# Two latent tails cut 1 + 3 blocks instead of 2 + 2, with PEER's row gathers in a new order

## The chip, the cores and the metric

One NeuronCore of one Trainium2 chip runs the whole program. The metric is the device time of that core in microseconds (us), as the median of several executions. The profile is one further execution, recorded instruction by instruction.

## What is computed

Two layers of a backbone run over 512 latent tokens and 256 context tokens, 1024 channels, all in fp32. Cut to what matters here:

```
for l in range(2):
    o_lat, o_ctx = token_mixer(modulate(x), modulate(ctx), ...)   # conv, retention, mLSTM, windowed attention
        # merge: acc = sum_i sigmoid(gate_i) * (ys[i] @ w_branch[i]);  out = acc @ w_out
    x = x + ga1 * o_lat
    x = x + ga2 * peer_ffn(modulate(x, norm2_g[l], sh2, sc2), ...)
    if l == 0: ctx = the same for ctx
return rmsnorm(x, final_g)

def peer_ffn(h, wq, keys, u, v):           # blocks of 128 tokens
    q = h @ wq                             # 8 heads x 2 halves x 128
    s = q . keys                           # 128 keys for each half
    top 16 per half -> 256 candidates -> top 16 experts per head (of 16384)
    act  = gelu(h . u[expert])             # 128 rows of u for each token
    out += (gate * act) @ v[expert]        # 128 rows of v for each token
```

## The kernel before

A block is 128 tokens: the context has two, the latents four. The program is four passes through the mixer, one after the other: `C0` (layer 0, context), `L0` (layer 0, latents), `C1` (layer 1, context, states only) and `L1` (layer 1, latents). `C0`, `L0` and `L1` end in PEER calls `PC0` (2 blocks, numbered 0 and 1), `PL0` (4 blocks, 2 to 5) and `PL1` (4 blocks, 6 to 9).

**The tail.** Behind the mixer's branches stands a tail of three stages, `merge`, `out` and `query`, done for one half of the blocks at a time: `halves_of(p)` (L73) gives `(0, 1), (2, 3)` for latents, and `pass_stages` makes stages `merge0, out0, query0, merge1, out1, query1`. `merge_part` (TensorE L1174) goes over 16 pairs (j, branch). Each pair has a gate weight (1 MB) and a branch weight (512 KB), and for both of its column halves m eight gate matmuls (L1182) and four branch matmuls (L1188) with the half's tokens as the moving operand, W = 256 columns. `outp` (L1196) multiplies each block with four 1 MB weights (L1216), adds the residual, makes the second RMSNorm (VectorE and ScalarE), stores the normalised rows `h2`, and transposes them. `query` (L1227) makes 16 chunks of the query (L1236, eight matmuls of 256 columns, 1 MB of weight for two chunks) and the scores (L1249). An fp32 matmul leaves two records in the trace. Weights come in through one queue (SyncE, L3039) into a ring of 4 slots; a slot is loaded again when TensorE has used it. All weights of the tail are read once for each half, 16 x 1.5 + 4 + 8 = 36 MB.

In `l0` twelve of the sixteen pairs of `merge0` are woven with the late convolution (`late_units`), in `l1` twelve with the attention (`attn_mix`); the last four are the stage itself.

**Routing.** The scores of a half's first block in `query0` are searched at once by VectorE (`top_keys`, `candidates`, two heads behind each group of four chunks). The scores of the other blocks go to memory, and VectorE searches them a head at a time between the dot products of the PEER block before (`route_part`, L2142). `centre`, `pick_keys` and `experts` then make the indices.

**PEER.** A block has 128 slots (`SLOTS`). For each slot GpSimd issues a gather of 128 rows of `u` and one of 128 rows of `v` (L3009), 4 KB a row, 512 KB in all. VectorE makes one dot product for each `u` gather (L2197). TensorE sums each `v` gather into PSUM with four narrow matmuls (`v_sum`, L1266 to L1275, eight records). `gather_tables` (L112) gives each gather one of 8 row buffers, and of 14 from the second block of a latent call on (6 of them lie in the mixer's memory), and says which reader must be done before. The order is, for `it` from the first block to one behind the last: slot by slot, `u` of block `it` and `v` of block `it - 1`. So the first 128 steps gather `u` alone, the last 128 `v` alone.

**What runs beside what.** Each engine's program is one fixed list. `side_by_side` (L725) puts steps of the PEER call between the pieces of another generator, in proportion to the cost that this yields (TensorE's estimates):

```
side_by_side("l0", mixer(L0), side, ROUTE + 3 * SLOTS, 0.9, costs)   # side = peer(PC0)
side_by_side("t0", tail(L0, 1), side, ROUTE + SLOTS, 1.0, costs)     # side = peer(PL0)
side_by_side("c1", mixer(C1), side, 3 * SLOTS, 1.0, costs)
side_by_side("t1", tail(L1, 1), side, ROUTE + SLOTS, 1.0, costs)     # side = peer(PL1)
```

`ROUTE` = 4 steps stand for the last part of routing. `mixer(L0)` and `mixer(L1)` end with their tail of half 0. GpSimd isn't part of these lists: it goes through the gathers in their order and waits for buffers, for the indices of a block (`idxu`, `idxt`), and once for the end of `query1` before `u` of a call's second block. `L1`'s mixer starts when `PL0` has ended.

Of the kernel before, what the change touches and what calls it, by code (L numbers as in the profile page):

```python
# [72 lines left out]
def halves_of(p):  # L73

    return [(x, x + 1) for x in range(0, p.n // P, 2)]
# [35 lines left out]

def gather_tables():  # L112

    buffer, before = {}, {}
    for call in (PC0, PL0, PL1):
        last, reader = call.first + len(call.blocks) - 1, {}
        for it in range(call.first, last + 2):
            if it == call.first:
                u_ring, v_ring = range(8), ()
            elif it == last + 1:  # L120
                u_ring, v_ring = (), range(8 if call is PC0 else 14)
            elif call is PC0:
                u_ring, v_ring = (0, 1, 2, 3), (4, 5, 6, 7)
            else:
                u_ring, v_ring = (0, 1, 2, 3, 8, 9, 10, 11), (4, 5, 6, 7, 12, 13)
            for n in range(SLOTS):
                for kind, ring, i, step in (("u", u_ring, it, "dot"), ("v", v_ring, it - 1, "v_summed")):
                    if call.first <= i <= last:
                        x = ring[n % len(ring)] if len(ring) in (4, 8, 14) else ring[((it - call.first) * SLOTS + n) % 6]
                        buffer[kind, i, n], before[kind, i, n] = x, reader.get(x)  # L130
                        reader[x] = (step, i, n)
    return buffer, before
# [3 lines left out]
ROUTE = 4  # L136
# [159 lines left out]
def query_units(p, f):  # L296

    order = []
    for c in range(2 * HEADS):
        order.append(("chunk", c))  # L300
        if f == 0 and c % 4 == 1 and c > 4:
            order.append(("score", 0, c // 4 - 1))
    if f == 0:
        order.append(("score", 0, 3))
    return order + [("score", x, g) for x in halves_of(p)[f][1 if f == 0 else 0:] for g in range(4)]
# [44 lines left out]
def build(nc, ins, out, known):  # L350
    ctx = ExitStack()
    with ctx:
# [189 lines left out]
        ACC, H2, XO = lay(4 * BB * LAT, KD * W, 2 * D, 2 * D)  # L542
        ACC, H2, XO = rows4(ACC, KD), rows4(H2, 2), rows4(XO, 2)
        GS, PRD = H2[:, 0, 0:3 * W].rearrange("p (b t) -> p b t", b=3), H2[:, 0, 3 * W:4 * W]
        ODD = MA[:, 0:4 * BB * LAT].rearrange("p (c f t) -> p c f t", c=16, f=2)

        def out_work():

            ga, sc2, sh2, g2 = (ODD[:, 4 * x:4 * x + 4, 0, :] for x in range(4))
            return ga, sc2, sh2, g2, g2[:, 0:2, :]  # L550

        H2T = HT.rearrange("p (k f t) -> p k f t", k=KD, f=2)[:, :, 0, :]

        def query_rows(c):
            return ACC[:, c, :] if c < KD else H2[:, (c - KD) // 4, (c - KD) % 4 * W:(c - KD) % 4 * W + W]

        def score_work(x):

            if x == 0:
                return SCO.rearrange("p (g c t) -> p g c t", g=4, c=2)  # L560
            if x == 2:
                return ODD[:, 0:8, 1, :].rearrange("p (g c) t -> p g c t", g=4)
            return MA[:, 10 * D + 2 * D:10 * D + 4 * D].rearrange("p (g c t) -> p g c t", g=4, c=2)
# [184 lines left out]
        def _(eng):  # L748
# [425 lines left out]
            def merge_part(p, f, part):  # L1174
                pn, half = p.name, slice(f * W, (f + 1) * W)
                for j, i_ in part:
                    wg = weight(("gate", pn, f, j, i_))
                    wb = weight(("branch", pn, f, j, i_), BB)
                    for m in range(2):
                        b = bank(("gate", pn, f, j, i_, m))  # L1180
                        for k in range(KD):
                            i = mm(b[:, 0:W], wg[:, k, m * P:(m + 1) * P], HTk(p)[:, k, half], start=(k == 0),  # L1182
                                   stop=(k == KD - 1))
                        i.then_inc(*mn.step("full", ("gate", pn, f, j, i_, m)))
                        yield 3.4
                        b = bank(("branch", pn, f, j, i_, m))
                        for k in range(BB):
                            i = mm(b[:, 0:W], wb[:, k, m * P:(m + 1) * P], YS(p, i_)[:, k, half], start=(k == 0),  # L1188
                                   stop=(k == BB - 1))
# [4 lines left out]
                        yield 1.8  # L1194

            def outp(p, f):  # L1196
                mn.stage((f"out{f}", p.name))
                pn = p.name

                def transposed(x, t):  # L1200

                    for half in range(2):
                        b = bank(("hT", pn, t, half))
                        eng.wait_ge(*at("h2", pn, t))
                        for k in range(4):
                            kk = half * 4 + k
                            i = turn(b[:, k * P:(k + 1) * P], H2[:, x % 2, kk * P:(kk + 1) * P], ident)
                        i.then_inc(*mn.step("full", ("hT", pn, t, half)))

                for x in halves_of(p)[f]:  # L1210
                    t = blocks_of(p)[x]
                    for j in range(D // W):
                        w = weight(("out", pn, f, j))
                        b = bank(("out", pn, j, t))
                        for k in range(KD):
                            i = mm(b[:, 0:W], ACC[:, k, x % 2 * P:(x % 2 + 1) * P], w[:, k, :], start=(k == 0), stop=(k == KD - 1))  # L1216
                        i.then_inc(*mn.step("full", ("out", pn, j, t)))
                        if x % 2:
                            used(("out", pn, f, j))
                        yield 3.5  # L1220
                    if x % 2:
                        transposed(x - 1, t - 1)
                        yield 2.2
                transposed(x, t)
                yield 2.2

            def query(p, f):  # L1227
                mn.stage((f"query{f}", p.name))
                pn = p.name
                for what, *n in query_units(p, f):  # L1230
                    if what == "chunk":
# [3 lines left out]
                        for k in range(KD):  # L1235
                            i = mm(b[:, 0:W], w[:, k, m * P:(m + 1) * P], H2T[:, k, :], start=(k == 0), stop=(k == KD - 1))  # L1236
# [3 lines left out]
                        yield 3.5  # L1240
                        continue
                    x, g = n
                    t = blocks_of(p)[x]
                    b = bank(("score", pn, t, g))
                    for y in range(4):
                        hc = 4 * g + y
                        if x % 2 == 0:
                            eng.wait_ge(*at("read", ("wq", pn, f, hc)))
                        i = mm(b[:, y * KEYS:(y + 1) * KEYS], query_rows(hc)[:, x % 2 * P:(x % 2 + 1) * P],  # L1249
# [1938 lines left out]
```

## Time and profile before

| | |
|---|---|
| median of 3 runs | 6093.1 us (6083.96 to 6100.71) |
| time of the profiled execution | 6088.19 us |
| its span, first to last instruction | 6086.3 us |
| busy: TensorE / VectorE / GpSimd / ScalarE | 4101.5 / 3226.0 / 2754.4 / 702.4 us |
| mean granted TensorE clock | 0.763 |
| gathers | 2560, 1384.49 MB, 60.1% of the 16 DMA engines' span |
| `merge0` of `l0`; of `l1` (with attention) | 1583 to 1848; 4103 to 4373 |
| window `t0`; the rest of `PL0` beside `C1` and alone | 1974 to 2320; 2320 to 3592 |
| window `t1`; the rest of `PL1` alone | 4494 to 4844; 4844 to 6066 |

Busy time is the sum over an engine's instructions without overlaps. The DMA share is the mean busy share of the core's 16 DMA engines and can come out slightly over 1. A granted clock of 1.00 is 2.4 GHz, 0.50 is 1.2 GHz. In a timeline row, the number in brackets is the engine's idle time before the group and what ended it.

### The profile page before, as it was taken

The numbers are of one execution on the slowest core, as the hardware profiler recorded it, in microseconds if no ns is written. First come the engines' busy times: TensorE is split into PE (matmuls) and PEld (weight loads), VectorE is DVE, ScalarE is ACT, GpSimd is POOL, SyncE is SP. The second block draws the span as 40 slices with busy tenths as digits, with TensorE's granted clock in tenths as the row PEclk, the third lists the DMA queues.
The fourth block names the chain that finished last, engine by engine and source line by source line (L and its number), as shares of the span: only waits on it lengthen the run. The fifth ranks groups of instructions, "written<-read, shape, count | busy, mean of one in ns | idle before, by whom it ended". The sixth has DMA issues, their size and how long they took to land. (4 is left out here: it accounts for less than half of the span.)

```text
span 6086.3 us, 64932 instructions
## 1 busy us (share of the span) xinstructions
PE 4101.5 (67%) x23632; PEld 2449.2 (40%) x23632; DVE 3226.0 (53%) x7722; ACT 702.4 (12%) x1562; POOL 2754.4 (45%) x2606
## 2 busy tenths in 40 slices
PE   5889676668998885554454569898878633334447
PEld 4767544335566663221021125457767500000001
DVE  3522698657434875756544217443268665664430
ACT  1221112123111001000000011233100100000000
POOL 0000144566330445777777730000014477777775
PEclk9999787779999987665555679999989855555555
DMA  6655466899885899999999961112559899999999
GB/s 224 207 164 179 156 234 227 303 322 335 275 293 188 311 331 332 386 363 402 384 400 409 404 269 51 52 46 73 161 190 333 322 379 364 395 378 397 409 402 380
DMA packets 721230, 1739.23 MB, mean 286 GB/s; under 512 B 88912, under 2 KB 371408, under 8 KB 719248
## 3 DMA queue, kind: packets, MB, share of 16 engines
q0 software_dynamic: 380032, 1384.49, 60.1%
q1 hardware_dynamic: 314896, 304.03, 16.0%
q10 hardware_dynamic: 25984, 46.56, 2.2%
q8 instruction: 188, 3.08, 0.2%
q14 instruction: 130, 1.06, 0.1%
HBM read 1706.98 MB, written 27.89 MB: 285 GB/s over the span
## 5 line engine op out<-in xcount | busy, mean ns | idle before, releaser
L3009 POOL DMA_INDIRECT arena<-in_peer_u,arena x1280 | 1408.2, 1100 | 2259.4 <-DVE arena L2107 1093.7
L1275 PE MATMUL bank<-arena 128*32 128x256 f32 x10240 | 1199.9, 563 | 1348.5 <-DMA arena<-in_peer_v,arena 1339.7
L2197 DVE CUSTOM_DVE_ANT_0 arena<-arena 128x1024 f32<-128x1024 f32 x1280 | 1540.6, 1222 | 908.6 <-DMA arena<-in_peer_u,arena 885.6
L3009 POOL DMA_INDIRECT arena<-in_peer_v,arena x1280 | 1319.4, 1031 | 627.7 <-issue 310.9
L1275 PEld LDWEIGHTS bank<-arena 128*32 128x32 f32 x10240 | 252.0, 131 | 2250.6 <-DMA arena<-in_peer_v,arena 2135.9
L784 PE MATMUL bank<-arena 128*128 128x512 f32 (+1 forms) x1856 | 731.6, 550 | 27.9 <-issue 13.1
L1182 PE MATMUL bank<-arena 128*128 128x256 f32 x2560 | 620.3, 398 | 89.0 <-issue 56.2
L1182 PEld LDWEIGHTS bank<-arena 128*128 128x128 f32 x2560 | 506.8, 200 | 184.7 <-issue 99.6
L784 PEld LDWEIGHTS bank<-arena 128*128 128x128 f32 x1856 | 372.8, 206 | 338.2 <-issue 315.0
L1188 PE MATMUL bank<-arena 128*128 128x256 f32 x1280 | 306.6, 382 | 2.3 <-ACT arena L2736 2.3
L1236 PE MATMUL bank<-arena 128*128 128x256 f32 x1280 | 290.1, 390 | 17.8 <-issue 17.8
L1236 PEld LDWEIGHTS bank<-arena 128*128 128x128 f32 x1280 | 249.7, 196 | 55.1 <-issue 19.7
L1188 PEld LDWEIGHTS bank<-arena 128*128 128x128 f32 x1280 | 239.1, 190 | 47.8 <-ACT arena L2736 12.7
L754 PE MATMUL bank<-arena 128*128 128x128 f32 x408 | 94.3, 359 | 219.7 <-DVE arena L1434 123.9
L1965 DVE SCALAR_TENSOR_TENSOR arena<-arena,bank 128x256 f32<-128x256 f32 x120 | 50.3, 419 | 328.2 <-PE bank L1188 293.0
L1507 DVE SCALAR_TENSOR_TENSOR arena<-arena 128x512 f32<-128x512 f32 (+1 forms) x360 | 213.8, 658 | 5.8 <-DVE arena L1507 0.4
L795 PE MATMUL bank<-arena 128*128 128x256 f32 (+1 forms) x960 | 214.9, 384 | 1.4 <-ACT arena L2522 1.4
L2819 ACT ACTIVATE arena<-arena 128x16 f32<-128x16 f32 x80 | 17.2, 216 | 1628.8 <-DVE arena L2197 1571.5
L795 PEld LDWEIGHTS bank<-arena 128*128 128x128 f32 x960 | 180.5, 207 | 38.6 <-issue 16.0
L2167 DVE TENSOR_TENSOR arena<-bank,arena 128x512 f32<-128x512 f32 x20 | 12.9, 685 | 338.3 <-PE bank L1275 338.3
L754 PEld LDWEIGHTS bank<-arena 128*128 128x128 f32 x408 | 64.7, 185 | 259.5 <-issue 169.3
L2971 POOL DMA_DIRECT2D arena<-in_mod_w x20 | 15.0, 755 | 323.1 <-PE bank L822 323.1
(269 smaller groups left out, 3844.5 us busy)
## 6 DMA issues: line engine op xcount, KB each, us to landing
arena<-in_w_in SPq DMA_DIRECT2D x152, 1024.0 KB, 6.9
arena<-in_mod_w POOLq DMA_DIRECT2D x20, 2048.0 KB, 11.5
arena<-in_peer_wq SPq DMA_DIRECT2D x40, 1024.0 KB, 5.5
arena<-in_w_branch SPq DMA_DIRECT2D x60, 512.0 KB
arena<-in_w_out SPq DMA_DIRECT2D x20, 1024.0 KB, 6.8
arena<-in_peer_u,arena POOLq DMA_INDIRECT x1280
arena<-in_peer_v,arena POOLq DMA_INDIRECT x1280
arena<-in_w_branch SPq DMA_DIRECT2D x40, 256.0 KB
```

Of the source, the lines that this page charges most:

```text
L754: return nc.tensor.transpose(dst, src, eye)
L784: i = mm(b[:, 0:p.n], w[:, k, m * P:(m + 1) * P], HTk(p)[:, k, :], start=(k == 0), stop=(k == KD - 1))
L795: i = mm(b[:, 0:n], HTk(p)[:, k, t * P:(t + 1) * P], w[:, k, c0:c0 + n], start=(k == 0), stop=(k == KD - 1))
L1182: i = mm(b[:, 0:W], wg[:, k, m * P:(m + 1) * P], HTk(p)[:, k, half], start=(k == 0), stop=(k == KD - 1))
L1188: i = mm(b[:, 0:W], wb[:, k, m * P:(m + 1) * P], YS(p, i_)[:, k, half], start=(k == 0), stop=(k == BB - 1))
L1236: i = mm(b[:, 0:W], w[:, k, m * P:(m + 1) * P], H2T[:, k, :], start=(k == 0), stop=(k == KD - 1))
L1275: i = mm(banks[6 + g // 2][32 * j:32 * j + 32, (g % 2) * W:(g % 2 + 1) * W], G["ws"][:, g, 32 * m:32 * m + 32], G["row"][ROW_BUFFER["v", i ...
L1507: v.scalar_tensor_tensor(y[:, m, :], cp[:, m, j:j + p.n], tap, y[:, m, :], ALU.mult, ALU.add)\
L1965: v.scalar_tensor_tensor(PRD, g, 1.0, b[:, 0:W], ALU.add, ALU.mult).then_inc(*mn.step("read", ("branch", pn, f, j, i_, m)))
L2197: v.tensor_tensor_reduce(u, u, G["h2"][it % 2], 1.0, 0.0, ALU.mult, ALU.add, G["dots"][:, n:n + 1]).then_inc(*pr.step("dot", it, n))
L2819: act(G["act"][:, hs], G["dots"][:, hs], ACT.Gelu).then_inc(*pr.step("gelu", it, h))
L3009: fl.done(eng.indirect_dma_start(G["row"][x], None, table, bass.IndirectOffsetOnAxis(ids[:, n:n + 1], 0)), f"row_landed{x}", (kind + "_lan ...
```

## The change

1. `halves_of` gives `(0,)` and `(1, 2, 3)` for the latent passes. The moving operand of merge and query is 128 columns wide in half 0 and 384 in half 1; the context pass keeps its one half of 256. `query_units` now puts the scores of each half's first block between the chunks, so VectorE searches two blocks (0 and 1) in the query stages, and `route_part` only blocks 2 and 3.
2. `peer_steps` writes PEER's order out as a list. For a latent call: 4 routing steps; 128 `u` of the first block; its first 64 `v` alone; 32 more `v`, every eighth with a routing step of the second block; 128 `u` of the second block with a `v` of the first at every fourth; then `u` of a block and `v` of the one before, as until now. In `t0` and `t1` 4 + 128 + 64 steps stand beside the tail instead of 4 + 128, in `c1` 32 + 384 instead of 384. `PC0` keeps its order.
3. The row buffers follow: 8 for `u` and `v` alike until the 96th `v`, then 8 and 6.
4. The memory of the tail is laid out anew (`tail_rows`), and the modulation rows and the first residual block are loaded ahead of the end of the merge (`out_rows_early`), the rest behind it (`out_rows_late`).

```diff
 def halves_of(p):
-    return [(x, x + 1) for x in range(0, p.n // P, 2)]
+    return [(0,), tuple(range(1, p.n // P))] if p.t0 else [tuple(range(p.n // P))]
...
+V_EARLY, V_LEAD = SLOTS // 2, SLOTS // 4
+def led(call):
+    return (call.first,) if call is PC0 else (call.first, call.first + 1)
+def peer_steps(call):
+    first, last, steps = call.first, call.first + len(call.blocks) - 1, []
+    for s in range(ROUTE):
+        steps.append(((first, s), None, None))
+    for n in range(SLOTS):
+        steps.append((None, (first, n), None))
+    if call is not PC0:
+        for n in range(V_EARLY):
+            steps.append((None, None, (first, n)))
+        for n in range(V_LEAD):
+            s, now = divmod(n, V_LEAD // ROUTE)
+            steps.append((None if now else (first + 1, s), None, (first, V_EARLY + n)))
+        for n in range(SLOTS):
+            v, now = divmod(n, 4)
+            steps.append((None, (first + 1, n), (first, V_EARLY + V_LEAD + v) if now == 3 else None))
+    for it in range(led(call)[-1] + 1, last + 2):
+        for n in range(SLOTS):
+            steps.append((None, (it, n) if it <= last else None, (it - 1, n)))
+    return steps
...
-                            i = mm(b[:, 0:W], wg[:, k, m * P:(m + 1) * P], HTk(p)[:, k, half], start=(k == 0),
+                            i = mm(b[:, 0:n], wg[:, k, m * P:(m + 1) * P], HTk(p)[:, k, half], start=(k == 0),
...
-                        yield 3.4
+                        yield n / W * 3.4
...
-            side_by_side("t0", tail(L0, 1), side, ROUTE + SLOTS, 1.0, costs)
+            side_by_side("t0", tail(L0, 1), side, ROUTE + SLOTS + V_EARLY, 1.0, costs)
-            side_by_side("c1", mixer(C1), side, 3 * SLOTS, 1.0, costs)
+            side_by_side("c1", mixer(C1), side, V_LEAD + 3 * SLOTS, 1.0, costs)
-            side_by_side("t1", tail(L1, 1), side, ROUTE + SLOTS, 1.0, costs)
+            side_by_side("t1", tail(L1, 1), side, ROUTE + SLOTS + V_EARLY, 1.0, costs)
...
+            def out_rows_early(p, f):
+                T, first_it = tail_rows(p, f), CALLS[p.name].first
+                ended = STAGES[STAGES.index((f"merge{f}", p.name)) - 1]
+                for e in ENG:
+                    eng.wait_ge(*at("end", e, ended))
+                eng.wait_ge(*at("mod_stored", p.l, 1))
+                eng.wait_ge(*at("experts", first_it if f else first_it - 1))
+                dma(T["ga"], mod_piece(p, 2), "out_gate", ("out_gate", p.name, f))
+                residual_in(p, f, halves_of(p)[f][0])
+                dma(T["g2"], norm_row(p), "out_rows")
+                if f == 0:
+                    dma(T["sc2"], mod_piece(p, 4), "out_rows")
+                    dma(T["sh2"], mod_piece(p, 3), "out_rows", ("out_rows", p.name, f))
```

## Rows read from the trace of the kernel before

**Rows 1.** The page's part 5: line, engine, operation | busy us, mean ns of one.

```profile
L2197 DVE CUSTOM_DVE_ANT_0 arena<-arena 128x1024 f32<-128x1024 f32 x1280 | 1540.6, 1222 | 908.6 <-DMA arena<-in_peer_u,arena 885.6
```

**Rows 2.** Busy time by stretch (us): each engine (instructions), granted clock, DMA share, GB/s.

```profile
730.00:1080.00 350.00, 250.22 (x806) 152.62 (x804) 296.51 (x764) 63.71 (x124) 150.07 (x125) 0.82 0.68 233
1080.00:1505.00 425.00, 311.76 (x2131) 177.89 (x2133) 263.83 (x610) 100.57 (x224) 268.56 (x253) 0.83 0.93 329
...
1583.00:1848.00 265.00, 264.49 (x1606) 172.31 (x1607) 116.42 (x189) 21.71 (x45) 95.58 (x95) 1.00 0.87 289
...
1974.00:2320.00 346.00, 281.96 (x1235) 241.97 (x1235) 266.45 (x621) 33.92 (x73) 150.10 (x128) 0.90 0.93 326
...
4103.00:4315.00 212.00, 188.40 (x1290) 161.59 (x1289) 65.83 (x169) 64.43 (x171) 0.00 (x0) 0.98 0.24 75
...
4373.00:4414.00 41.00, 30.89 (x145) 26.77 (x145) 15.24 (x28) 5.07 (x9) 0.00 (x0) 0.92 0.84 282
4414.00:4494.00 80.00, 67.05 (x320) 59.58 (x320) 45.02 (x208) 7.84 (x16) 0.00 (x0) 0.91 0.33 106
4494.00:4716.00 222.00, 186.67 (x769) 157.98 (x769) 181.75 (x464) 15.66 (x39) 97.84 (x84) 0.90 0.92 318
...
4844.00:5190.00 346.00, 130.24 (x965) 24.47 (x969) 206.39 (x482) 4.38 (x10) 271.50 (x245) 0.50 0.99 374
5190.00:5893.00 703.00, 285.14 (x2107) 53.44 (x2107) 385.70 (x779) 7.13 (x21) 540.00 (x527) 0.50 1.02 397
```

**Rows 3.** Timeline of GpSimd's gathers where `t0` and `t1` end and at each call's end.

```profile
2325.84 0.94 POOL L3009 DMA_INDIRECT arena<-in_peer_v,arena  x1 [0.30 <-issue]
...
3576.21 0.93 POOL L3009 DMA_INDIRECT arena<-in_peer_v,arena  x1 [0.30 <-issue]
...
4842.86 0.94 POOL L3009 DMA_INDIRECT arena<-in_peer_u,arena  x1 [10.70 <-ACTq L2803]
4844.10 0.94 POOL L3009 DMA_INDIRECT arena<-in_peer_v,arena  x1 [0.30 <-issue]
...
6050.48 0.93 POOL L3009 DMA_INDIRECT arena<-in_peer_v,arena  x1 [0.30 <-issue]
```

**Rows 4.** Timeline of TensorE, matmuls of 256 and of 128 columns in layer 1's tails.

```profile
4140.03 2.05 PE L1137 MATMUL bank<-arena 128*128 128x128 f32 x16 [1.29 <-ACT arena L2698]
...
4436.42 1.05 PE L1249 MATMUL bank<-arena 128*128 128x128 f32 x8
4437.31 7.94 PE L1236 MATMUL bank<-arena 128*128 128x256 f32 x36
...
4580.63 3.62 PE L1182 MATMUL bank<-arena 128*128 128x256 f32 x16
4584.08 1.89 PE L1188 MATMUL bank<-arena 128*128 128x256 f32 x8
```

**Rows 5.** TensorE's groups in 1583 to 1848, and its waits in 1080 to 1505.

```profile
L1275 PE MATMUL bank<-arena 128*32 128x256 f32 x760 | 55.7, 388 | 0.0
...
PE bank L1275 <- DMA arena<-in_peer_v,arena: 84.4, 46, 5.2
```

**Rows 6.** Weight loads: issues in 4110 to 4375 (with queue) and 4494 to 4713, us to landing.

```profile
q1 hardware_dynamic: 24468, 24.50, 30.8%
...
arena<-in_w_in SPq DMA_DIRECT2D x14, 1024.0 KB, 5.4
...
arena<-in_w_in SPq DMA_DIRECT2D x14, 1024.0 KB, 10.0
```

**Rows 7.** Timeline of VectorE: one routing group in `query0`, then the indices behind it.

```profile
4438.20 0.49 DVE L2020 MAX8 arena<-arena 128x8 f32<-128x128 f32 x2 [1.16 <-ACT arena L2793]
...
4450.43 0.42 DVE L2118 COPY arena<-bank 128x256 f32<-128x256 f32 x1
...
4498.64 0.23 DVE L2062 TENSOR_TENSOR arena<-arena 128x128 f32<-128x128 f32 x1
...
4515.97 0.23 DVE L2092 CAST arena<-arena 128x128 uint32<-128x128 f32 x1
```

More of the change, by code:

```diff
@@ L115, in gather_tables @@
     for call in (PC0, PL0, PL1):
[L116 to L123, printed above, removed]
-            else:
[L125 to L131, printed above, removed]
+        last, reader, given = call.first + len(call.blocks) - 1, {}, {"u": 0, "v": 0}
+        for _, u, v in peer_steps(call):
+            if call is PC0:
+                u_ring = range(8) if u and u[0] == call.first else (0, 1, 2, 3)
+                v_ring = (4, 5, 6, 7) if u else range(8)
+            elif u and u[0] == call.first or v and v[0] == call.first and v[1] < V_EARLY + V_LEAD:
+                u_ring, v_ring = range(8), range(8)
+            else:
+                u_ring = (0, 1, 2, 3, 8, 9, 10, 11)
+                v_ring = range(14) if v and v[0] == last else (4, 5, 6, 7, 12, 13)
+            for kind, row, ring, step in (("u", u, u_ring, "dot"), ("v", v, v_ring, "v_summed")):
+                if row:
+                    x = ring[given[kind] % len(ring)]
+                    given[kind] += 1
+                    buffer[(kind,) + row], before[(kind,) + row] = x, reader.get(x)
+                    reader[x] = (step,) + row
     return buffer, before
 ROW_BUFFER, READ_BEFORE = gather_tables()
-ROUTE = 4
 CONST = {}
@@ L1174, in merge_part @@
             def merge_part(p, f, part):
-                pn, half = p.name, slice(f * W, (f + 1) * W)
+                pn, half, n = p.name, span(p, f), width(p, f)
                 for j, i_ in part:
@@ new lines, in peer @@
+                for lead, u, v in peer_steps(call):
+                    if lead:
+                        it, s = lead
+                        if s == 0 and it > call.first:
+                            rows_in(it)
+                        if s == 2:
+                            gate_exp(pr, G, it)
+                    if u:
+                        it, n = u
+                        h, k = divmod(n, TOPK)
+                        if k == TOPK - 1:
+                            gelu(it, h)
+                        if it + 1 <= last and it + 1 not in led(call):
+                            if n == (HEADS - 2) * TOPK:
+                                gate_exp(pr, G, it + 1)
+                            if n == 0:
+                                scores_in(it + 1)
+                            if n == 4:
+                                rows_in(it + 1)
+                        if n == SLOTS - 1:
+                            spread(it)
+                    if v:
+                        it, n = v
+                        if n == 2 and it > call.first:
+                            x_out(it - 1)
+                        if n == 24:
+                            x_in(it)
+                    yield 0
@@ L2998, in gathers @@
                 G = peer_work(call)
-                last = call.first + len(call.blocks) - 1
                 def gather(kind, it, n):
```

409 lines of the change are left out of this document (211 added, 198 removed).

## The prediction

> **What bounds the kernel now.** I cut the span into stages with the table of busy time by stretch, read what bounds each, then went to the timelines of TensorE, GpSimd and VectorE for prices. Three regimes appear [rows 2]. In PEER alone (4844 to 5893) the DMA share is 0.99 to 1.02 while TensorE is busy for 38 to 41% at half clock: the gathers' bytes set the pace. From the first `v` gather behind `t1` to the last 895 intervals lie in 6050.48 - 4844.10 = 1206.4 us, 1.348 us each; in layer 0 it is 1250.4 us, 1.397 each, beside `C1`'s weights [rows 3]. In `merge0` of layer 0 TensorE is busy for 264.5 of 265 us. In `t0` and `t1` both are nearly full: DMA 0.92 to 0.93, TensorE 81 to 84% [rows 2]. In layer 1's `merge0` no gather runs, DMA share 0.24. So a gather row taken out of the stretches behind the tails is worth 1.348 us, provided that the tails don't grow by as much. Both layers are symmetrical here: `L1` starts when `PL0` has ended, and the program ends with `PL1`.
>
> **Part 1, matmul widths.** TensorE's pitch at full clock: 16 records of 256 columns take 4584.08 - 4580.63 = 3.45 us, 0.216 each; 8 records of 128 columns take 0.89 us, 0.111 each [rows 4]. So time goes with columns; 384 I take as 0.322 (256 plus half of it). A half has 16 x 2 x 12 x 2 = 768 merge records, 16 x 8 x 2 = 256 query records, 64 `out` records for each block. Half 0 loses 768 x 0.105 + 256 x 0.105 + 64 x 0.216 = 81 + 27 + 14 = 122 us of TensorE; half 1 gains the same. Widths alone are neutral.
>
> The Trainium skill (TensorE: Matmul & The Clock Gate, Back-to-back issue gap) says otherwise for narrow matmuls: with a weight load for each, 128 columns sustain about 81 ns instead of an isolated 56. By that ratio the 1024 narrow records would cost 1024 x 0.111 x 0.45 = 51 us a layer. The trace's 0.111 already has a weight load for each record, so I go by the trace; that rule's outcome is rival 3.
>
> **Part 2, half 0 gets shorter.** How much of the 122 us arrives?
> - Layer 1, twelve pairs woven with attention: 12 x 48 x 0.105 = 60 us less TensorE work over 16 units. But TensorE already waits 1.29 us for ScalarE's exponential in a unit [rows 4], and that chain doesn't shrink. A unit is about 13 us now (212 / 16, rows 2); the scores are issued one unit ahead of the transposes that wait, so the chain from scores to probabilities is about as long as a unit, 13 us. With only 4 us of merge and 3.3 of attention of TensorE's own in a unit, two units can't be shorter than 13 + 3.3 + 4, one not than about 10. I take 40 us, bounds 20 and 60.
> - The last four pairs: 20 us less; but a pair of 1.5 MB must land in the 5.3 us of the pair before, and 1 MB alone takes 5.4 us [rows 6]. 18 us.
> - `out`: 14 us less; four weights are needed in 14 us, behind 2.5 MB of early rows. I take 8, bounds 0 and 14.
> - `query`: 27 us less for TensorE, but VectorE's search of two heads is 4450.43 - 4438.20 = 12.2 us [rows 7] and four chunks are now only 7.1 us. The stage becomes six chunks, then 4 x 12.2 us and some copies: about 63 us of 80 [rows 2]. 17 us.
> Sum for layer 1: 83 us earlier. In layer 0 the woven pairs are TensorE-bound, so all 81 us come; its window "l0" also gets 17% denser in PEER steps (388 steps over about 700 units of yielded cost instead of 820, counted in the code), so some 49 `v` sums at 55.7 / 95 = 0.59 us [rows 5] leave `merge0`. With what DMA (0.87 there) takes back I count 93, with `out` 10 and `query` 17: 120. Against it stands the place that the steps move to: 1080 to 1505, DMA 0.93, would shrink to 363 us and can't get under 0.93 x 425 / 0.98 = 403; with VectorE at 85% ahead of it [rows 2] I charge 33 us, bounds 0 and 60. Layer 0: 87 us earlier.
>
> **Part 3, `t0` and `t1` get longer.** TensorE's pure work now: 768 + 256 + 128 records at 0.216 and some 100 narrow ones = 260 of 350 us; 90 us are overhead. After: 768 x 0.322 + 192 x 0.216 + 256 x 0.322 + 144 x 0.111 = 247 + 41 + 82 + 16 = 386, and 64 `v` sums x 0.59 = 38: 424. Of the overhead these stay: the start behind the routing (12), the last block's norm (17), half-clock stretches (8; 0.90 over 222 us now, rows 2), a new wait of 7 where the first `v_sum` stands in TensorE's list until the last dots are weighed, turned and spread; and late weights. Those shrink: a weight lands in 10.0 us here instead of 5.4 [rows 6], a pair of TensorE work was 10.4 us and becomes 15.5. I take 12. Sum 56, the window 480 us, +130. DMA has for it 200 gathers x 1.348 = 270 and 36 MB at 24.5 MB in 0.308 x 265 us [rows 6] = 120 and some rows: 400 of 480, no denser than now. Bounds 445 and 520. VectorE loses the routing of the second block there (about 50 us, see below) and gets it back in `query1`, 12.2 us for each 20.6 us of chunks: hidden. The residual and modulation loads behind `merge1` are hidden by the first block's 14 us of `out`.
>
> **Part 4, what is left behind the tails.** GpSimd doesn't stop at the end of `t1` any more (10.70 us idle now, rows 3): 64 `v` are summed, 8 more in buffers, so 824 of 1024 gathers remain instead of 896: 72 x 1.348 = 97 us less in each call. The 24 `v` left before `u` of the second block cover 32 us; `centre` to `experts` needs 4516.2 - 4498.6 = 17.6 us [rows 7]. Hidden, if the search of its last heads ends with `query1`. Without that cover the 10.7 us gap returns.
> The second block's `u` now go with only a quarter of `v`: 160 gathers, 216 us. VectorE has in it all that it has in 4844 to 5190 now, 206 us [rows 2]: 128 dots at 1.23 [rows 1] and about 50 us of routing in lumps of up to 8 us. At 0.96 of the pace, with 8 buffers of `u`, I charge 20 us; in layer 0, where `C1` adds some 0.1 us a step, 22. Bounds 0 and 50.
>
> **The sum.** Layer 1: -83 + 130 - 97 + 20 = -30. Layer 0: -87 + 130 - 97 + 22 = -32. Together -62 on 6088.2, the profiled execution; that stands 5 us under the median of 6093.1. Forecast **6031 us**, own range 5995 to 6070.
>
> **Rivals.**
> 1. *Only bytes count.* The windows grow to 455 only (wide matmuls hide every weight, `v` sums fill waits), and VectorE's lumps vanish in the buffers. -25 x 2 - 42: **5939 us**. For it: of VectorE's 908.6 us idle ahead of dots 885.6 are put down to gathers not landed [rows 1], so it has mostly been ahead of them. Against: it has been so at 60% of the pace, not at 96%.
> 2. *VectorE and the pace of steps take it back* (the change does nothing). In the second block's `u` part the dots fall behind their buffers by 50 instead of 21 us in each call: +58, **6089 us**. For it: no such dense part exists today. Against: the 885.6 us of rows 1.
> 3. *Narrow matmuls cost what the page has.* 51 us a layer in half 0, none given back in half 1: **6133 us**. For it only that rule; against it 0.111 against 0.216 [rows 4].
> 4. *`v` sums stop the mixer.* In `t0` and `t1` each `v_sum` stands in TensorE's list ahead of the tail's matmuls. If the gathers, held back by the weights, are always the later ones, each costs a full 1.348 instead of 0.59: +49 in each window, **6129 us**. From 31 us a window (0.48 us a sum) it eats the gain. For it: 84.4 us of such waits in 1080 to 1505 [rows 5], 155 sums, 0.54 each. Against: there two gathers fall on a step, here one, on a step of over 2 us.
>
> **Chances.** Forecast 0.46, rival 1 0.31, rival 2 0.12, rival 3 0.02, rival 4 0.09. A measurement of this kernel tells 0.3% (18 us) from no change. Faster by more: the forecast and rival 1 nearly whole, 0.77; within 0.3%: rival 2 and the forecast's edge, 0.12; slower: rivals 3 and 4, 0.11. The range for 8 in 10 leaves out rivals 3 and 4, the far end of 1 and a sliver of 2: 5940 to 6095.
>
> **What would show it.** The first `u` gather of `PL1` near 4400 (the indices come at 4516.2 now [rows 7], less 83 and 32); with less, part 2 is wrong. `t1` of about 480 us with a DMA share of 0.8 to 0.9 and hardly a wait for weights in `merge1`; waits of the `v` matmuls on DMA there mean rival 4. A continuous row of gathers across the end of `query1`. Some 236 us instead of 216 for the second block's `u`, with VectorE full. Then the old pace of 1.35 us a gather. The prediction is wrong above all if half 0's 120 us don't arrive, or if the window grows by 160 rather than 130.

## The result, and the profile after

The changed kernel took 6158.24 us (median of 4, 6152.26 to 6170.6), the kernel before beside it 6090.83 (4 runs): ratio 1.0112, 95% interval 1.009 to 1.0134. It is 67 us slower where 62 us faster was forecast. The profiled execution has a span of 6150.5 us against 6086.3, 64.2 more.

Busy time by stretch of the changed kernel; columns as in [rows 2]:

```profile
1046.00:1473.00 427.00, 294.00 (x1669) 153.92 (x1670) 231.84 (x529) 70.12 (x140) 268.65 (x254) 0.75 0.92 328
1473.00:1666.00 193.00, 167.42 (x1566) 102.60 (x1564) 71.19 (x163) 64.09 (x161) 81.84 (x85) 1.00 0.75 258
1666.00:1849.00 183.00, 163.25 (x1253) 116.63 (x1246) 111.60 (x193) 17.86 (x44) 51.16 (x45) 0.96 0.84 283
1947.00:2442.00 495.00, 442.13 (x1850) 264.16 (x1850) 268.31 (x602) 40.90 (x79) 221.62 (x199) 0.95 0.87 305
2442.00:3670.00 1228.00, 586.19 (x4034) 199.15 (x4034) 642.13 (x1411) 51.57 (x106) 888.39 (x825) 0.57 0.97 371
2512.00:2787.00 275.00, 100.71 (x498) 60.35 (x490) 222.84 (x546) 20.15 (x38) 197.73 (x160) 0.63 0.89 328
4183.00:4383.00 200.00, 166.73 (x1559) 155.51 (x1557) 67.64 (x191) 66.67 (x185) 0.00 (x0) 0.97 0.43 135
...
4407.00:4477.00 70.00, 39.11 (x288) 38.27 (x288) 43.71 (x208) 4.62 (x12) 0.00 (x0) 0.77 0.33 106
4477.00:4771.00 294.00, 259.92 (x762) 150.46 (x763) 184.98 (x326) 19.20 (x41) 150.49 (x122) 0.93 0.87 304
...
4851.00:4977.00 126.00, 125.34 (x753) 70.32 (x754) 45.85 (x208) 10.52 (x19) 46.20 (x50) 0.98 0.76 250
...
5017.00:5262.00 245.00, 39.11 (x302) 7.64 (x298) 205.99 (x490) 4.40 (x10) 192.36 (x161) 0.51 0.94 345
```

The stage borders in both traces give this account, in us, with the terms of the prediction beside it:

| | before | after | moved | forecast |
|---|---|---|---|---|
| start of `t0` (first gate matmul of half 1) | 1974 | 1947 | -27 | -87 |
| window `t0` | 346 | 495 | +149 | +130 |
| rest of `PL0`, beside `C1` and alone | 1272 | 1228 | -44 | -75 |
| `L1`'s mixer to its first gate matmul | 511 | 513 | +2 | 0 |
| layer 1, `merge0` to `query0` | 391 | 294 | -97 | -83 |
| window `t1` | 350 | 500 | +150 | +130 |
| rest of `PL1` to its last sum | 1222 | 1153 | -69 | -77 |
| **sum** | | | **+64** | **-62** |

So layer 1 gained 14 us, and layer 0 lost 78. Of the 126 us between forecast and measurement 60 are in the first row, 39 in the two windows and 31 behind `t0`; layer 1's other rows are 6 us better than forecast, and `L1`'s mixer took 2 more. In the first row the miss begins here: the first gate matmul of layer 0 comes at 1666.2 instead of 1582.9, 83 us later, though nothing in that part of the mixer was changed.

### The profile page after: what moved, and what is told of

Read it like the earlier page. It is cut to its first block and busy times, and to the rows that moved or that the text cites. A ratio compares the mean times of both kernels' runs of the same rounds, so it can differ in the third digit from the quotient of the medians.

```text
span 6150.5 us, 64955 instructions
## 1 busy us (share of the span) xinstructions
PE 4066.5 (66%) x23632; PEld 2300.8 (37%) x23632; DVE 3230.0 (53%) x7724; ACT 713.8 (12%) x1569; POOL 2797.5 (45%) x2606
## 5 line engine op out<-in xcount | busy, mean ns | idle before, releaser
L3065 POOL DMA_INDIRECT arena<-in_peer_u,arena x1280 | 1440.0, 1125 | 2104.2 <-DVE arena L2156 1014.6
L1325 PE MATMUL bank<-arena 128*32 128x256 f32 x10240 | 1153.7, 548 | 1388.1 <-DMA arena<-in_peer_v,arena 1381.9
L1231 PE MATMUL bank<-arena 128*128 128x384 f32 (+2 forms) x2560 | 618.2, 397 | 115.4 <-issue 72.8
L1231 PEld LDWEIGHTS bank<-arena 128*128 128x128 f32 x2560 | 430.4, 200 | 289.2 <-issue 139.0
L833 PEld LDWEIGHTS bank<-arena 128*128 128x128 f32 x1856 | 366.7, 203 | 345.3 <-issue 324.2
L1286 PE MATMUL bank<-arena 128*128 128x128 f32 (+2 forms) x1280 | 306.1, 401 | 19.0 <-issue 16.9
L1237 PE MATMUL bank<-arena 128*128 128x128 f32 (+2 forms) x1280 | 307.8, 384 | 1.8 <-ACT arena L2785 1.8
L1286 PEld LDWEIGHTS bank<-arena 128*128 128x128 f32 x1280 | 216.4, 206 | 100.8 <-issue 35.8
L1237 PEld LDWEIGHTS bank<-arena 128*128 128x128 f32 x1280 | 209.2, 192 | 86.2 <-ACT arena L2785 9.3
L2014 DVE SCALAR_TENSOR_TENSOR arena<-arena,bank 128x128 f32<-128x128 f32 (+2 forms) x120 | 50.5, 421 | 347.0 <-PE bank L1237 201.8
L844 PEld LDWEIGHTS bank<-arena 128*128 128x128 f32 x960 | 179.8, 206 | 38.3 <-issue 15.9
L2218 DVE TENSOR_TENSOR arena<-bank,arena 128x512 f32<-128x512 f32 x20 | 12.9, 686 | 342.0 <-PE bank L1325 342.0
L1266 PE MATMUL bank<-arena 128*128 128x256 f32 x640 | 147.8, 390 | 19.6 <-DMA arena<-in_w_out 17.2
```

Source lines behind the costliest of these rows:

```text
L833: i = mm(b[:, 0:p.n], w[:, k, m * P:(m + 1) * P], HTk(p)[:, k, :], start=(k == 0), stop=(k == KD - 1))
L844: i = mm(b[:, 0:n], HTk(p)[:, k, t * P:(t + 1) * P], w[:, k, c0:c0 + n], start=(k == 0), stop=(k == KD - 1))
L1231: i = mm(b[:, 0:n], wg[:, k, m * P:(m + 1) * P], HTk(p)[:, k, half], start=(k == 0), stop=(k == KD - 1))
L1237: i = mm(b[:, 0:n], wb[:, k, m * P:(m + 1) * P], YS(p, i_)[:, k, half], start=(k == 0), stop=(k == BB - 1))
L1266: i = mm(b[:, 0:W], T["acc"][:, k, y * P:(y + 1) * P], w[:, k, :], start=(k == 0), stop=(k == KD - 1))
L1286: i = mm(b[:, 0:N], w[:, k, m * P:(m + 1) * P], T["h2t"][:, k, :], start=(k == 0), stop=(k == KD - 1))
```

## The experiments

Runs 1 to 4 were on a chip where the kernel before took 6087 us; the other eight where it took 6305 to 6307 us and a gather behind the tails about 1.47 us instead of 1.35. Ratios are always to the kernel before on the same chip, and whole times are compared on one chip alone. The lengths of the windows `t0` and `t1` are compared across chips below: run 9, on the slower one, has 494 and 500 us from the first gate matmul to the last score, the same as the changed kernel on the faster. Where no ratio is given there is one time.

**1. The old density of the context call in the changed kernel.** The number behind the steps is the share of the window over which they are spread: a smaller one sets them denser.

```diff
-            side_by_side("l0", mixer(L0), side, ROUTE + 3 * SLOTS, 0.9, costs)
+            side_by_side("l0", mixer(L0), side, ROUTE + 3 * SLOTS, 1.0, costs)
```

> The changed kernel, but PEER's steps of the context call are spread over the whole of the window l0 (share 1.0) instead of 0.9 of it. The yielded cost of that window is 778.4 units (912.2 before the change), so 388 steps over 778 units are nearly as thin as the old 388 over 821. My theory (the shorter tail squeezed the context call's gathers into a stretch that DMA already filled, which cost some 50 of the 60 us by which t0 starts later than forecast): t0's first merge matmul moves from 1947 to 1895-1925 and the whole gets 25 to 50 us faster than the changed kernel, ratio to the kernel before 1.003 to 1.008. Rival (the narrow tail itself is what arrives late, because of weights or of attention-like chains): t0 starts at 1940-1965, no gain or a loss, as v sums now fall into the tail. Second rival: v sums in tail 0 eat it, also no gain.

6136.89 us, ratio 1.008 (1.0056 to 1.0105). The first gate matmul came at 1623 instead of 1666, but `t0` started at 1936, 11 us ahead of the changed kernel and not 22 to 52: `merge0` took 198 instead of 183 us and `out0` and `query0` 114 instead of 98, since the `v` sums had moved there. The direction is that of the theory, the size at `t0` is under its range; the ratio is at the upper end of its range, and its interval overlaps that of the changed kernel. Of the 43 us gained ahead of the gates 32 were lost again in the tail, as the second rival had it.

**2. The new density in the kernel before, and nothing else.**

```diff
-            side_by_side("l0", mixer(L0), side, ROUTE + 3 * SLOTS, 0.9, costs)
+            side_by_side("l0", mixer(L0), side, ROUTE + 3 * SLOTS, 0.768, costs)
```

> The kernel before, with the share of window l0 lowered from 0.9 to 0.768, so that the context call's steps stand as densely as in the changed kernel (388 steps over 700 units of cost), nothing else. If the density costs 50 to 80 us ahead of the merge, merge0 of layer 0 starts at 1630-1665 instead of 1583, and part of that comes back in a merge with fewer v sums: t0 starts 15 to 50 us later than 1974 and the ratio is 1.003 to 1.008. If the density is harmless (rival): merge0 starts at 1583-1600 plus the v sums moved (25 us), t0 at 1965-1980 and the ratio is 0.998 to 1.001.

6153.9 us, ratio 1.0115 (1.0086 to 1.0143): as slow as the whole change, with old halves and old order, and beyond the 1.003 to 1.008 that I expected. Busy time by stretch of this kernel, columns as above:

```profile
1052.00:1479.00 427.00, 289.41 (x1669) 150.18 (x1670) 231.88 (x531) 70.03 (x140) 272.32 (x254) 0.75 0.91 328
1479.00:1675.00 196.00, 171.86 (x1566) 105.30 (x1564) 71.02 (x163) 64.10 (x161) 80.81 (x85) 0.97 0.75 254
1675.00:1908.00 233.00, 231.92 (x1256) 166.72 (x1249) 118.85 (x193) 21.24 (x44) 46.65 (x45) 1.00 0.68 219
```

The reader is to set its first row against the changed kernel's first (the same 427 us and 1669 records) and against 1080 to 1505 in [rows 2]: 425 us as well, the same 253 gathers, but 2131 TensorE records. The stretch in which the context call gathers `u` and `v` together took its 426 us here whether 2131 or 1669 records of TensorE stood in it. What the mixer doesn't get done there is done behind it: 196 us to the first gate matmul (at 1675) instead of 78. The first 128 `u` gathers end 27 us sooner (319 us from 733 instead of 346), so the gates come 92 us late and not 118. `merge0` gives 30 us of that back (233 instead of 262 to 265), as it has fewer sums. `t0` starts at 2033, 59 us late. TensorE's waits for `v` rows in the stretch from 1052 to 1479, to be set against [rows 5]:

```profile
PE bank L1275 <- DMA arena<-in_peer_v,arena: 125.3, 61, 7.1
```

**3. The second block's lead steps ahead of `C1`'s mixer.** GpSimd's timeline of the changed kernel behind `t0`, and VectorE's at the same place:

```profile
2442.12 0.94 POOL L3065 DMA_INDIRECT arena<-in_peer_v,arena  x1 [0.71 <-issue]
2470.49 0.94 POOL L3065 DMA_INDIRECT arena<-in_peer_v,arena  x1 [27.44 <-PE bank L1325]
```

```profile
2457.49 0.24 DVE L1464 SCALAR_TENSOR_TENSOR arena<-arena 128x8 f32<-128x8 f32 x2 [16.46 <-DMA arena<-mod_rows]
```

The gathers stop for 27 us: the next `v` sum is listed behind `C1`'s first norm, and that waits for the layer's vectors. I took this wait for a new one. It isn't: the kernel before stops at the same place.

```profile
2361.78 1.44 POOL L3009 DMA_INDIRECT arena<-in_peer_v,arena  x1 [20.70 <-PE bank L1275]
```

```diff
+            for _ in range(V_LEAD):
+                next(side)
-            side_by_side("c1", mixer(C1), side, V_LEAD + 3 * SLOTS, 1.0, costs)
+            side_by_side("c1", mixer(C1), side, 3 * SLOTS, 1.0, costs)
```

> The changed kernel, but the 32 v-only steps with the second block's routing stand ahead of C1's mixer instead of between its pieces (c1 then takes 3*SLOTS steps). Theory: in the changed kernel GpSimd stands still for 27 us behind t0, because its next v sum is listed behind C1's first norm, which waits for the layer's vectors (16.5 us of VectorE waiting on mod_rows); with the steps ahead of it the gathers go on, u of the second block starts at about 2490 instead of 2512 and the whole gets 10 to 28 us faster than the changed kernel, ratio 1.0065 to 1.0095. Rival: the vectors' loads come late anyhow and C1's norm then blocks the dense u part instead: the gap is only moved, ratio 1.010 to 1.012.

6152.86 us, ratio 1.0099 (1.0069 to 1.013), which doesn't tell it from the changed kernel. In the traces `u` of the second block starts at 2481 instead of 2512, but from the end of `t0` to the last `v` gather it is 1205 us instead of 1215. Of 31 us at the gap 10 arrive at the end: most of it was only moved, as the rival said. In its trace the `u` gathers now stop behind VectorE's dots, which the norm holds back:

```profile
2511.99 1.14 POOL L3071 DMA_INDIRECT arena<-in_peer_u,arena  x1 [18.55 <-DVE arena L2248]
```

**4. The new order with the old halves.** `peer_steps` without the early search: 64 `v` behind the first 128 `u`, then a `v` at every second `u` of the second block.

```diff
+        for n in range(V_EARLY):
+            steps.append((None, None, (first, n)))
+        for n in range(SLOTS):
+            v, now = divmod(n, 2)
+            steps.append((None, (first + 1, n), (first, V_EARLY + v) if now else None))
...
-            side_by_side("t1", tail(L1, 1), side, ROUTE + SLOTS, 1.0, costs)
+            side_by_side("t1", tail(L1, 1), side, ROUTE + SLOTS + V_EARLY, 1.0, costs)
```

> The kernel before with its two halves of two blocks each, and of the change only the new order: 64 v of the first block stand in t0 and t1 behind its u, and the other 64 go with u of the second block, one at every second slot. No early search of the second block. Sum from the rows: windows t0 and t1 get 64 v sums (0.5 to 0.6 us each, 32 to 38 us) and the wait of 7 us at the first of them, 40 to 50 us longer each; behind them 72 gathers fewer, 97 us less each. If the loss of the change lies in the 1+3 cut (my theory), this one is faster than the kernel before: 0.983 to 0.993. If v sums and gathers in the tails are what costs (rival), the windows grow by 80 or more and the ratio is 0.997 to 1.005.

6119.83 us, ratio 1.0069 (1.0042 to 1.0095). I had expected 0.983 to 0.993. My theory of the 1 + 3 cut as the only culprit fell. Both windows, from the first gate matmul to the last score, grew from 339 and 342 to 433, by 91 to 94 us for 64 sums, or 1.4 to 1.5 us each, and behind them 69 and 91 us were saved.

**5. The same with light weights.** Is it the weights' DMA? Of the gate, `out` and query weights of half 1 only an eighth is loaded; the kernel computes with stale values in their place.

```diff
+        for n, (name, parts) in enumerate(PLAN):
+            if name[1] in ("l0", "l1") and name[0] in ("gate", "out", "wq") and name[2] == 1:
+                (dst, src), = parts
+                PLAN[n] = (name, [((lambda w, dst=dst: dst(w)[:, 0:1, :]), src[:, 0:1, :])])
```

> order_alone (2 + 2 blocks, 64 early v), but in half 1 of both latent tails the gate, out and wq weights are loaded to one eighth only, so that part of the computation uses stale weights: the weights' DMA in t0 and t1 falls from 36 MB to about 11.5 MB. If DMA sets the 433 us of these windows (200 gathers x 1.348 = 270 and 120 us of weights, DMA nearly full), they fall to 340-370 us. If TensorE's own work and its waits for v sums set them (298 us of pure work), they stay above 400.

6295.23 us against 6306.9. The windows were still 420 and 422 us instead of 433. So the loading of the weights is worth 11 to 13 of the 91 to 94 us. TensorE's waits in `merge1` of layer 1, first with full, then with light weights (us in total, times, longest):

```profile
PE bank L1209 <- DMA arena<-in_w_branch: 29.2, 5, 9.1
PE bank L1209 <- DVE arena L1991: 18.5, 6, 5.6
```

```profile
PE bank L1213 <- DVE arena L1995: 40.2, 16, 5.7
```

The waits for weights go, and those for VectorE, which has to free the banks, take their place. It is busy there for 232.5 of 261 us with full and 222.4 of 249 with light weights, because 196 instead of 132 steps over the same tail bring the 128 dots, with the second block's search between them, into less of it.

**6. The early `v` behind the windows, in the changed kernel.**

```diff
-            side_by_side("t0", tail(L0, 1), side, ROUTE + SLOTS + V_EARLY, 1.0, costs)
+            side_by_side("t0", tail(L0, 1), side, ROUTE + SLOTS, 1.0, costs)
-            side_by_side("c1", mixer(C1), side, V_LEAD + 3 * SLOTS, 1.0, costs)
+            side_by_side("c1", mixer(C1), side, V_EARLY + V_LEAD + 3 * SLOTS, 1.0, costs)
```

> The changed kernel with the same list of PEER steps, but only 4 + 128 of them stand in t0 and t1; the 64 early v follow behind (in c1's window for layer 0, alone for layer 1). Theory A (a v in the tail costs PE and DMA time of the tail nearly as much as it saves behind): windows 45 to 75 us shorter than 495 and 500, the rest 86 us longer, in all 0 to 30 us slower than the changed kernel for both layers: ratio 1.010 to 1.017. Theory B (TensorE's fixed order makes each early v cost more than its 1.348 us, as order_alone's 91 us for 64 hint): windows over 86 us shorter, the whole 0 to 30 us faster than the changed kernel, ratio 1.005 to 1.011.

Ratio 1.01 (1.0083 to 1.0117), no different from the changed kernel. The windows are 423 and 425 us (first gate matmul to last score) instead of 494 and 500: 71 and 75 us for 64 `v`, 1.1 to 1.2 us each, which is theory A. `merge1` of layer 1 with the early `v` behind, to be set against 4477 to 4771 in the windows of the changed kernel above:

```profile
4573.00:4830.00 257.00, 249.13 (x762) 146.15 (x763) 140.16 (x247) 18.82 (x38) 90.48 (x84) 0.98 0.82 270
```

No `v` sum stands in either. The changed kernel's 37 us more go with 122 instead of 84 `u` gathers in the merge: TensorE's waits put down to issue, which is where late weights show (run 8), are 33.8 us there and 7.7 here, and the granted clock is 0.93 there and 0.98 here. The other half of the price lies in `out1` and `query1`.

**7. The cut alone.** PEER in its old order, the second block searched in `query1`, its last routing in four steps without gathers.

```diff
+    if call is not PC0:
+        for s in range(ROUTE):
+            steps.append(((first + 1, s), None, None))
+    for it in range(first + 1, last + 2):
```

> The 1 + 3 cut alone: PEER in its old order (128 u, then u and v slot by slot), but the second block is searched in query1, and its last routing (4 steps, 18 us) stands between the first 128 u and the rest with no gathers beside it. t0 and t1 carry 4 + 128 steps. Windows 430 to 455 us (386 of TensorE's pure work and 45 to 70 of pauses) instead of 346 and 350; tail 0 of layer 1 95 us shorter as in the changed kernel, of layer 0 only 27 because of the dense l0 window; behind the windows the old 1272 and 1222 plus 10 to 20 us for the routing gap. Sum: layer 0 +70 to +90, layer 1 +0 to +25: ratio 1.011 to 1.019. If it is no slower than the changed kernel (1.0112), the early v brought nothing.

Ratio 1.0099 (1.0082 to 1.0116); windows 422 us both, shorter than my 430 to 455. `t0` starts at 1959 for 1958 in run 6. The cut without any early `v` is as slow as the whole change: the early `v` brought nothing on balance. But it has a loss of its own: without `v` gathers to cover the second block's last routing, GpSimd stands still for 50.1 us in layer 0 and 38.7 in layer 1 (15.0 and 10.7 in the kernel before), where I had charged 10 to 20 us more.

**8. Light weights in the changed kernel.** The edit is that of run 5, put at the same place:

```diff
+            if name[1] in ("l0", "l1") and name[0] in ("gate", "out", "wq") and name[2] == 1:
+                PLAN[n] = (name, [((lambda w, dst=dst: dst(w)[:, 0:1, :]), src[:, 0:1, :])])
```

> The changed kernel, with gate, out and wq weights of half 1 of both latent tails loaded to one eighth only (that part then computes with stale weights). The changed kernel's windows were 495 and 500 us, in t1 TensorE idle 57 us of it, 46 put down to weights and to issue. If late weights are what lengthens them over my 480, they fall to 445 to 465. If not (order_light had stayed at 420 of 433), they stay above 485.

6233.07 us against 6304.59. The windows (to the last score) fell to 449 and 448 from 494 and 500. TensorE's first stretch of `t1` then is 247 us busy of 247, at full clock: the 768 x 0.322 us of the prediction. With full weights it is 294 us, 260 of them busy: the 47 us between are 34 of waiting and 13 of matmuls at a lower clock (granted 0.93 instead of 1.00). Behind the longest of these waits, 8.62 us, the next 16 records took 7.34 us instead of 5.16.

```profile
4520.00:4767.00 247.00, 247.00 (x764) 145.30 (x764) 185.09 (x325) 19.38 (x42) 145.42 (x122) 1.00 0.87 303
```

**9. Early sums with one narrow matmul of four.**

```diff
-                    for j in range(COLS):
+                    for j in range(1 if it in (PL0.first, PL1.first) and n < V_EARLY and 0 < m < 31 else COLS):
```

> The changed kernel, but of the first 64 v gathers of the latent calls 60 are summed with one of the four narrow matmuls (three quarters of their sum are left out); gathers and waits stay. v_late showed that each early v lengthens the window by 1.16 us. If TensorE's own time for the sums is it (0.5 to 0.6 us, of which three quarters go), the windows fall by 20 to 27 us to 468-480. If it is the wait for the rows or the paced order, they fall by less than 10.

6329.33 us against 6304.59. The windows stayed at 494 and 500 us. But it says nothing against TensorE's time, as the groups of `query1` show, changed kernel first:

```profile
L1325 PE MATMUL bank<-arena 128*32 128x256 f32 x401 | 27.0, 385 | 0.0
```

```profile
L1325 PE MATMUL bank<-arena 128*32 128x256 f32 x112 | 26.1, 385 | 0.0
```

112 records instead of 401 take nearly the same time: the four matmuls of a sum run beside each other, so leaving three out frees nothing. In the timelines the matmul behind a single sum starts 0.57 us after it with all four (4964.50 to 4965.07) and 0.55 with one (5059.94 to 5060.49). This test could not tell the two theories apart.

**10. and 11. The kernel before with a thinner context call.** If density costs, less of it should pay.

```diff
-            side_by_side("l0", mixer(L0), side, ROUTE + 3 * SLOTS, 0.9, costs)
+            side_by_side("l0", mixer(L0), side, ROUTE + 3 * SLOTS, 1.0, costs)
```

> The kernel before with the share of window l0 raised from 0.9 to 1.0: 912 / 388 = 2.35 units of mixer cost to a PEER step instead of 2.12. Runs so far fit a simple rule: the context call's first 260 steps (to its last u) take 770 us whatever stands between them (last u at 1473 to 1505 in five kernels), so what the mixer hasn't done by then comes behind, at about 1 us a unit. By that rule 260 x 0.24 = 61 units more are done by then: merge0 starts at 1525-1550 instead of 1583, v sums fall into out0 and query0 and cost 15 to 30 us there, and t0 starts 15 to 45 us ahead of 1974: ratio 0.993 to 0.998. Rival (the old share is at the bend, further thinning stretches the gathers themselves): u ends after 1530, t0 at 1965-1985, ratio 0.999 to 1.002.

> before_l0_thin once more, beside the kernel above and on another chip, since its first chip was 3.5% slower in all kernels: 0.992 to 0.997 if the gain isn't bound to that chip; 0.998 to 1.001 if the slower gathers there made it.

Ratios 0.9943 (0.9923 to 0.9963) and 0.9979 (0.9967 to 0.9991): faster both times, by 0.2 to 0.6%. The second ratio is above my 0.992 to 0.997, and both came at the slower pace of the gathers, so that neither says whether the gain is bound to it; only run 1, in the changed kernel, points the same way on the faster chip. The last `u` gather moved to 1557 and 1559 and the stretch to 452 us, so it isn't as rigid as my rule had it (1473 to 1519 in all the others but run 12's, and 442 us for the stretch in run 1), but the first gate matmul comes at 1562 to 1563 instead of 1610 (run 5, the same window `l0`, at the same pace).

**12. Layer 1 of the changed kernel, layer 0 of the kernel before with the thin call.** The core of the edit, against the changed kernel:

```diff
-    return [(0,), tuple(range(1, p.n // P))] if p.t0 else [tuple(range(p.n // P))]
+    if p.name == "l1":
+        return [(0,), tuple(range(1, p.n // P))]
+    return [(x, x + 1) for x in range(0, p.n // P, 2)]
...
-    return (call.first,) if call is PC0 else (call.first, call.first + 1)
+    return (call.first,) if call is not PL1 else (call.first, call.first + 1)
...
-    if call is not PC0:
+    if call is PL1:
         for n in range(V_EARLY):
...
-            side_by_side("l0", mixer(L0), side, ROUTE + 3 * SLOTS, 0.9, costs)
+            side_by_side("l0", mixer(L0), side, ROUTE + 3 * SLOTS, 1.0, costs)
...
-            side_by_side("t0", tail(L0, 1), side, ROUTE + SLOTS + V_EARLY, 1.0, costs)
+            side_by_side("t0", tail(L0, 1), side, ROUTE + SLOTS, 1.0, costs)
-            side_by_side("c1", mixer(C1), side, V_LEAD + 3 * SLOTS, 1.0, costs)
+            side_by_side("c1", mixer(C1), side, 3 * SLOTS, 1.0, costs)
```

> Layer 1 as in the changed kernel (1 + 3 blocks, 64 early v in t1), layer 0 as before the change (2 + 2, old order, old windows) with share 1.0 in window l0. From the traces: the changed kernel's layer 1, from its first gate matmul to the end, took 1947 us instead of 1963, 14 to 17 us less; before_l0_thin gave 0.9943. If the parts add up: 0.990 to 0.993, and 10 to 20 us faster than before_l0_thin on the same chip. Rival: layer 1's gain was chance or its own gap eats it: equal to before_l0_thin within 8 us.

6254.29 us against 6304.59, ratio 0.992 (0.9896 to 0.9943), and 39 us less than the thin kernel beside it, where I had expected 10 to 20. In the traces `merge0` of layer 1 to the end takes 2053 us against 2087 of the thin kernel. On this chip a gather row behind the tails costs more, so 72 fewer are worth about 106 us instead of 97; with that some 23 us were due and 33 came. This version is faster than the kernel before, and by its ratio than the changed one.

## Why the prediction was wrong, point by point

- **Widths (part 1): right.** In the changed kernel a group of 16 narrow records takes 1.95 us with its last one's tail, the next group follows 1.88 us later, with one wider gap in it, 0.117 each for 0.111; 16 gate records of 384 columns take 5.16 us (4486.50 to 4491.66), 0.322 each, and light weights gave 247 us for 768 records. Rival 3 is out: the trace agrees with columns alone, not with the Trainium skill's figure for narrow matmuls (TensorE: Matmul & The Clock Gate, Back-to-back issue gap).

```profile
4204.43 1.95 PE L1231 MATMUL bank<-arena 128*128 128x128 f32 x16
4206.31 0.49 PE L1156 MATMUL bank<-arena 64*128 64x128 f32 x4
```

- **Half 0 in layer 1 (part 2): right in sum**, 97 us for 83, with some luck in the terms. From the first gate matmul to the thirteenth pair's it is 167 us (4183.1 to 4350.2) instead of 227 (4103.2 to 4330.6): the woven pairs gave all 60 us of TensorE's work, the far bound, and not 40. The chain through the exponential, which I had as the limit of a unit, didn't bind; TensorE waits for it as before, 21.1 us in all for 21.3. The last four pairs gave 11 for 18, with 7.4 us of waits for weights, `out0` 15 for 8 and `query0` 11 for 17. `query0` is VectorE's now: 39 us of TensorE in 70.
- **Half 0 in layer 0 (part 2): the step that failed.** I took "for the place that the steps move to" 33 us, bounds 0 and 60, and set 93 us from `merge0` against it. The gate matmuls came 83 us late, and `merge0` gave 79 from its first gate matmul to its last; so `t0` started 27 us earlier, not 87. The mistake was to ask how far the stretch 1080 to 1505 could shrink towards 363 us. It didn't shrink: it took 427 us, and the mixer's work that the denser steps pushed out of it was added behind. In 260 steps this is (2.12 - 1.81) x 260 = 81 units of yielded cost; that a unit comes back as about one us fits the 83 and 92 us of two kernels and isn't shown by itself. Run 2 shows the density alone: +92 ahead of the gates and +59 at `t0`, nearly the 60 us of the first row. The sign that I had named, the first `u` gather of `PL1` near 4400, came at 4499.7. The 122 us that half 0 sheds were handed, by the share of 0.9, to a call that didn't go faster. What inside the stretch holds it wasn't separated: the DMA share is 0.92, but at 328 GB/s, where the gathers from 5250 us on move 394; and GpSimd waits 63 us of it for VectorE's dots, which free the buffers, for 79 in the kernel before.
- **Windows (part 3): the mechanism right, a term mis-sized.** 424 us of pure work and 56 of pauses were forecast; 495 and 500 came. The term is the late weights, taken as 12 us: in `t1` TensorE waits 33.8 us in the merge and 4.6 in `out1` for them, and the slower clock behind such waits, taken as 8, shows as busy time, 443 us for 424. Runs 6 and 8 show it from both sides (-37 us in the merge with thinner `u`, -47 with light weights, and -45 and -52 in whole windows). I had argued that these waits shrink because a pair got longer; those put down to issue in the merge had been 30.3 us and stayed. The wait at the first `v_sum` was 7.6 us for 7. The last block's norm took 9.7 for 17, and the start behind the routing, 12.9 us, lies ahead of the first gate matmul, outside the window that I counted it in.
- **Behind the windows (part 4): right in layer 1**, 69 us for 77: the gathers run on across the end of `query1` and the second block's `u` take 245 us for 236. That last number came near by luck: I had put it down to a full VectorE, but VectorE was busy 206 of the 245 us and GpSimd waited only 3.6 for its dots; what held the gathers there is open. In layer 0 it is 44 for 75. The 27 us behind `C1`'s norm, which I hadn't listed, are only part of this: the kernel before had 20.7 of them, and run 3 says that some 10 count. The second block's `u` took 275 us for 238, and in it GpSimd once stood still for 21 us, because VectorE's next dot was listed behind pieces of `C1` that waited themselves; no stop in that part was over 4.3 us before.

```profile
2713.74 5.99 POOL L3065 DMA_INDIRECT arena<-in_peer_u,arena  x1 [21.18 <-DVE arena L2246]
```

- **The rivals and the balance.** None of the four names the failed step. Rival 1's windows of 455 us didn't come. Rival 2's mechanism shows in layer 0 alone, where GpSimd waits 29.5 us for dots in the second block's `u` (3.6 in layer 1). Rival 4 wanted 529 us and TensorE waiting for `v` rows; none of its waits in `t1` is put down to them. Its supporting figure was misread, too: the 84.4 us in 1080 to 1505 fall on 125 sums (1000 records), 0.68 each, not on 155. What holds of it is that an early `v` costs 1.1 to 1.2 us in the windows and gives back 1.35 or less. Half of that isn't the sum itself but the steps' greater density in the merge.

## What to carry to other kernels

When work is spread over a window in proportion to cost, a shorter window is a denser one: ask which stretch of it is already paced by the spread work, and count what is pushed out of there at full price. Gathers put into an idle share of DMA are paid by what shares it, here the weights, and by the banks that VectorE frees: a row gathered early cost 1.1 to 1.2 us in the changed kernel's windows and 1.4 to 1.5 in run 4's, where one gathered later costs 1.35. And try the spread's own knob before rearranging: it alone gave 0.2 to 0.6% here, on the slower chip.

## What the runs showed of the hardware

One of four narrow matmuls on its own column strip takes as long as all four: 26.1 us for 112 records against 27.0 for 401. And the same kernel took 6087 us on one chip and 6305 on another, with about 1.47 instead of 1.35 us to a gather in the part that the gathers pace; windows that TensorE paces were as long on both (494 and 500 us).
